# Gated attention scores counted from the middle of 128-token blocks in a two-layer encoder kernel

## The reference, cut to what matters

```python
def gla_scan(q, k, v, g):                      # per head: dk = 128, dv = 256, GLA_CHUNK = 64
    def step(state, inp):
        qc, kc, vc, gc = inp
        gcum = jnp.cumsum(gc, axis=1)
        q_t = qc * jnp.exp(gcum)
        k_t = kc * jnp.exp(-gcum)
        att = jnp.where(causal, jnp.einsum('blhk,bshk->blsh', q_t, k_t), 0.0)
        o = jnp.einsum('blsh,bshv->blhv', att, vc) + jnp.einsum('blhk,bhkv->blhv', q_t, state)
        g_end = gcum[:, -1]
        state = state * jnp.exp(g_end)[..., None] + ...

# gla_mixer: gk is the log gate / 16, q is scaled by 128 ** -0.5, four heads, two directions
o = gla_scan(q, k, v, gk[:, :, 0]) + flip_seq(gla_scan(flip_seq(q), ..., flip_seq(gk[:, :, 1])))
```

## Time and profile before

| what | value |
|---|---|
| median of three runs | 1341.2 us |
| the profiled execution | 1341.43 us, with a span of 1339.6 us |
| PE busy | 1320.0 us, 99% of the span |
| DVE, ACT, POOL busy | 777.4, 641.8, 621.8 us |
| granted PE clock | 0.998 of 2.4 GHz |

### The profile page before, as it was taken

How to read it: one execution, slowest core, us unless ns; L and a number is a source line. 1 busy time by engine, 2 the same in 40 slices (tenths; PEclk the granted TensorE clock), 3 DMA queues, 4 the chain that set the end, 5 groups by cost and what they waited for, 6 DMA issues and landing times.

```text
span 1339.6 us, 16496 instructions
## 1 busy us (share of the span) xinstructions
PE 1320.0 (99%) x6630; PEld 1119.0 (84%) x6630; DVE 777.4 (58%) x890; ACT 641.8 (48%) x1033; POOL 621.8 (46%) x294
## 2 busy tenths in 40 slices
PE   7999999999999999999999999999999999999997
PEld 6878878888898888888889888898998888888887
DVE  5857386840079998885002753386279988882002
ACT  5654787653355444443233576454554544443221
POOL 3344561245424644445553364554535544445551
PEclk9999999999999999999999999999999999999999
DMA  6332111123223332333333223301323333333331
GB/s 206 95 113 85 51 37 40 63 79 98 92 85 103 97 95 94 94 93 100 94 94 103 96 79 95 95 16 63 112 95 95 95 94 98 102 93 88 100 87 63
DMA packets 41452, 119.78 MB, mean 89 GB/s; under 512 B 4384, under 2 KB 12960, under 8 KB 41376
## 3 DMA queue, kind: packets, MB, share of 16 engines
q1 hardware_dynamic: 40160, 116.34, 28.5%
q10 hardware_dynamic: 1216, 2.38, 0.6%
HBM read 116.35 MB, written 2.23 MB: 89 GB/s over the span
## 4 chain that ended last, share of the span: by engine, by line
PE 93%; DVE 4%; ACT 1%; issue 1%; DMA 0%; ACTq 0%; DVEq 0%
PE bank L336 26%; PE bank L337 26%; PE bank L338 26%; PE bank L1774 1%; PE bank L1775 1%; PE bank L1773 1%; PE bank L2077 1%; PE bank L2059 1%; PE bank L1506 1%; PE bank L1509 1%; PE bank L1325 1%; PE bank L387 1%; PE bank L1292 1%; PE bank L1536 1%; DVE sqacc L663 1%
## 5 line engine op out<-in xcount | busy, mean ns | idle before, releaser
L319 POOL TENSOR_TENSOR wlo<-raw,whi 128x1024 fp32r<-128x1024 f32 (+2 forms) x215 | 531.1, 2483 | 633.9 <-ACT whi L313 633.8
L336 PE MATMUL bank<-xw_hi,whi 128*128 128x512 f32 (+1 forms) x1280 | 478.0, 373 | 8.6 <-DVE xw_lo L646 8.1
L338 PE MATMUL bank<-xw_hi,wlo 128*128 128x512 f32 (+1 forms) x1280 | 473.8, 370 | 0.0
L337 PE MATMUL bank<-xw_lo,whi 128*128 128x512 f32 (+1 forms) x1280 | 473.7, 370 | 0.0
L313 ACT ACTIVATE whi<-raw 128x1024 fp32r<-128x1024 f32 (+2 forms) x217 | 221.5, 1025 | 208.0 <-DMA raw<-in_fout 112.2
L336 PEld LDWEIGHTS bank<-xw_hi,whi 128*128 128x128 f32 x1280 | 242.5, 189 | 50.3 <-issue 8.9
L338 PEld LDWEIGHTS bank<-xw_hi,wlo 128*128 128x128 f32 x1280 | 242.3, 189 | 41.1
L337 PEld LDWEIGHTS bank<-xw_lo,whi 128*128 128x128 f32 x1280 | 242.5, 189 | 39.8 <-issue 0.2
L596 DVE RECIPROCAL small<-small 128x2 f32<-128x2 f32 x8 | 1.3, 165 | 315.1 <-ACT small L521 313.7
L715 DVE SCALAR_TENSOR_TENSOR cbuf<-ubuf,par,cbuf 128x510 f32<-128x510 f32 x100 | 168.7, 1687 | 3.5
L711 DVE SCALAR_TENSOR_TENSOR cbuf<-ubuf,par,cbuf 128x510 f32<-128x510 f32 x100 | 144.6, 1446 | 4.7 <-ACT cbuf L844 4.1
(11 more groups left out here) (278 smaller groups left out, 1453.9 us busy)
## 6 DMA issues: line engine op xcount, KB each, us to landing
raw<-in_fin SPq DMA_DIRECT2D x88, 512.0 KB, 3.6
raw<-in_fout SPq DMA_DIRECT2D x32, 448.0 KB, 3.3
raw<-in_gin SPq DMA_DIRECT2D x25, 512.0 KB, 3.6
raw<-in_hin SPq DMA_DIRECT2D x24, 512.0 KB, 3.7
raw<-in_hout SPq DMA_DIRECT2D x16, 512.0 KB, 3.6
raw<-in_fout SPq DMA_DIRECT2D x16, 512.0 KB, 3.6
raw<-in_gout SPq DMA_DIRECT2D x8, 512.0 KB, 3.9
xres<-in_x SPq DMA_DIRECT2D x8, 256.0 KB, 5.8
```

The lines of the kernel that those rows point to most:

```text
L319: engine.tensor_tensor(wlo[s][:, 0:n], raw[s][:, 0:n], whi[s][:, 0:n].bitcast(F32), ALU.subtract).then_inc(w_lo, 1)
L336: first = nc.tensor.matmul(out_ap, wh, ah, start=start, stop=False)
L337: nc.tensor.matmul(out_ap, wh, al, start=False, stop=False)
L338: return first, nc.tensor.matmul(out_ap, wl, ah, start=False, stop=stop)
```

## The change

It has five parts.

1. The running sum `gl` of every gate is counted from the middle of each 128-token block and no longer from the start of each 64-token chunk: `dve_from_middle` copies the eight chunk ends into `ends` (new L1848) and subtracts them from the chunks on one side of the middle (new L1852). One set of keys then serves all 128 queries of its block. The copies `kk`, their carries and zeros go. `dve_keys` is one multiplication into `ek` (new L1949), `scores` has two matmuls of 128 query columns and one cross matmul a request (all new L1991), and `dve_carries` is one addition.
2. Six buffers of `qt`, `ek` and `qx` where there were four (`AHEAD`). The exponentials of pairs 4 and 5 are written in stage gin, behind the split of one weight block, and POOL makes the queries of pairs 0 to 5 there, one pair after each of the last six blocks.
3. The factor 128 ** -0.5 is no longer in the mask and the copy, but in the exponent of `qt`, as a bias in a spare column of `small`, set by a memset.
4. Direction 1's diagonal scores go into `att` with `copy_predicated` under a mask, two instructions where there were two multiplications and two additions. The masks are 1 + identity (upper triangle with 2 on the diagonal) and the strict lower triangle.
5. The order on ACT in stage gla: three cross copies come before the table of Exp, and `outs(0)` is taken apart. Some semaphores are merged (`wgk_in`, `gmask_in`, `tri_in` into `gla_in`; `rope_in` into `cst_in`; `last_t` into `last_x`; `last_stored` into `out_stored`).

```diff
+AHEAD = 6
         def dve_gate_weights(dve):
-            dve.wait_ge(sem("wgk_in"), 16)
+            dve.wait_ge(sem("gla_in"), 48)
...
         def pe_hin(pe):
-                    pe.wait_ge(sem("cst_in"), 16)
+                    pe.wait_ge(sem("cst_in"), 32)
...
         def act_gin(act):
-            act.wait_ge(sem("carry_set"), CARRIES)
+            act.wait_ge(sem("carry_set"), 2)
             nc.scalar.activation(carry[:], carry[:], ACT.Exp, scale=GK_NORM).then_inc(sem("carry_exp"), 1)
+            act.wait_ge(sem("gate_mid"), G0)
             for n in range(4):
+                act_gate_exps(act, n)
+            his(act, base + 1 + 2 * G0)
+            for n in range(4, AHEAD):
                 act_gate_exps(act, n)
...
+        def dve_from_middle(dve, t):
+            d = t // GLA_HEADS
+            at, last = slice(t * NREQ * NCH, (t + 1) * NREQ * NCH), 0 if d else CH - 1
+            dve.wait_ge(sem("gate_scan"), t + 1)
+            nc.vector.tensor_copy(ends[:, at].unsqueeze(2), chunks_of(t)[:, :, last:last + 1]).then_inc(
+                sem("gate_ends"), 1)
+            dve.wait_ge(sem("gate_ends"), t + 1)
+            early = chunks_of(t)[:, d::2]
+            nc.vector.tensor_tensor(early, early, ends[:, at][:, d::2].unsqueeze(2).broadcast_to([P, NREQ * NCH // 2, CH]),
+                                    ALU.subtract).then_inc(sem("gate_mid"), 1)
...
         def dve_gin(dve):
                     if t >= GLA_HEADS:
                         least(t, ft)
+                    if ft:
+                        dve_from_middle(dve, t - 1)
                     dve.wait_ge(sem("gate_act"), 3 * t + 3)
                     dve.wait_ge(sem("gate_min"), t + 1)
                     nc.vector.tensor_tensor(ubuf[0][:], ubuf[0][:], cbuf[1][:], ALU.subtract).then_inc(
...
         def dve_keys(dve, n):
+            nc.vector.tensor_tensor(ek[n % AHEAD][:], ck(gqkv, 4 + n // 2), ek[n % AHEAD][:], ALU.mult).then_inc(
+                sem("gla_kk"), 1)
...
         def pe_gla(pe):
-                    for c in range(NCH):
-                        s = c // 2
-                        nc.tensor.matmul(out[:, s * SEQ + c * CH:s * SEQ + (c + 1) * CH],
-                                         kks(n)[:, r, c * SEQ + s * P:c * SEQ + (s + 1) * P],
-                                         qt[n % 4][:, r * SEQ + c * CH:r * SEQ + (c + 1) * CH], start=True, stop=True)
...
+                    for s in range(2):
+                        against(s, qt[n % AHEAD][:, r * SEQ + s * P:r * SEQ + (s + 1) * P], s)
+                    last = against(d, of_request(qx[n % AHEAD], r, P), 1 - d)
...
         def dve_gla(dve):
+                        nc.vector.copy_predicated(own[r], mask, blocks(sbank(d, r)[:])).then_inc(sem("gla_db"), 1)
```

More of the change, by code:

```diff
@@ L131, in build_program @@
         with ExitStack() as s:
-            kk1 = sb("kk1", NREQ * NCH * SEQ, F32, s)
+            sb("to_cbuf2", 2 * T, F32, s)
+            qx4, qx5 = (sb(f"qx{i}", NREQ * P, F32, s) for i in (4, 5))
         cbuf = [sb(f"cbuf{i}", T) for i in range(4)]
@@ L1869, in dve_gin @@
+        def dve_carries(dve):
+            dve.wait_ge(sem("gate_ends"), G0)
+            nc.vector.memset(small[:, 6:7], math.log(QG)).then_inc(sem("carry_set"), 1)
+            by_chunk = ends[:].rearrange("p (i c) -> p i c", c=NCH)
+            nc.vector.tensor_tensor(carry[:].unsqueeze(2), by_chunk[:, :, 1:2], by_chunk[:, :, 2:3], ALU.add).then_inc(
+                sem("carry_set"), 1)
         def dve_gin(dve):
@@ L1977, in dve_zero_keys @@
-        def dve_zero_keys(dve, n):
-            d = n % 2
-            for c in ((0, 2) if d == 0 else (1, 3)):
-                s0 = CH * (c + 1) if d == 0 else CH * (c - 1)
-                nc.vector.memset(kks(n)[:, :, c * SEQ + s0:c * SEQ + s0 + CH], 0.0).then_inc(sem("kk_zero"), 1)
+            if n >= AHEAD:
+                act.wait_ge(sem("gla_s"), n - AHEAD + 1)
+            f = slice((d * GLA_HEADS + hd) * T, (d * GLA_HEADS + hd + 1) * T)
+            nc.scalar.activation(qt[n % AHEAD][:], gl[:, f], ACT.Exp, bias=small[:, 6:7], scale=GK_NORM).then_inc(sem("gla_e"), 1)
@@ L1995, in dve_keys @@
-            step = SEQ + CH
-            if d == 0:
-                own = kks(n)[:, :, 0:3 * step].rearrange("p r (c y) -> p r c y", y=step)[:, :, :, 0:CH]
-                first, other = 0, 3
-            else:
-                own = kks(n)[:, :, CH:].rearrange("p r (c y) -> p r c y", y=step)[:, :, :, SEQ:]
-                first, other = 1, 0
-            for to, c in ((own, slice(first, first + 3)),
-                          (kks(n)[:, :, other * step:other * step + CH].unsqueeze(2), slice(other, other + 1))):
-                nc.vector.tensor_tensor(to, k[:, :, c], e[:, :, c], ALU.mult).then_inc(sem("gla_kk"), 1)
```

214 lines of the change are left out of this document (67 added, 147 removed).

## The result

The changed kernel takes 1333.48 us in the median of 4 runs (1333.04 to 1334.40), the kernel before 1341.01 beside it (1340.36 to 1341.83): a ratio of 0.9944, 95% interval 0.9932 to 0.9956, clear of no change. Five more runs of it gave 1333.86. I had given 1335.8, with 1334.2 as the lower end. The profiled run took 1333.35 us, its span is 1331.5 (1339.6 before).

The account below looks back on a forecast made before the run. PE, busy for 99% of the span, was taken to bound the kernel. 1341.43 - 6.6 (gla: 6.2 scores, 0.4 waits) + 1.1 (gate 3) = 1335.9, given as 1335.8 for a median; range 1334.2 to 1338.5.

Parts of the forecast that it names:

- Scores: PE's scores in gla: a request falls from 1.12 to 0.72 us, leaving PE 6.2 us less to do.
- The passage of 0.17: PE's scores: the time from one request's last record to the next request's start, 0.17 us against steps of 0.11.
- Rival 2: All 96 score records: 128 columns cost twice the 64, 0.21 us, so the time is 1343.2; chance 0.04.
- The predicated copy: DVE in gla: a predicated copy of 256 elements takes 0.38 us like the masking multiplication, bounds 0.3 and 0.7.
- Waits in gla: PE in gla: new waits of 0.4 us against 0.8 that go, so waits give back 0.4 us.
- Gate 3: PE in gin: a new wait of 1.1 us for gate 2's minimum, since POOL's split delays DVE's scan; bounds 0 and 3.4.
- rival 1: DVE's scan gets the seam ahead of POOL's split, so no wait at gate 3: 1334.7 us; chance 0.14.
- The collision at 775 to 777: DVE in gin: the new subtraction meets POOL's split of 775.50 to 777.91 and ends at about 778.4.
- Edits at no cost: End of gin, pairs 4 and 5's exponentials, POOL's queries, bias, masks, semaphores, ACT's order: 0 us, 0.2 either way.

Follow-up runs that it names:

- e5: Changed kernel with direction 1's own scores placed by a masking multiplication and an addition instead of the predicated copy: 1335.21 us, 0.9961 of the kernel before.
- e1: Changed kernel with each 128 x 128 diagonal score matmul issued as two of 64 columns: 1340.30 us, 0.9995 of the kernel before.
- e3: Changed kernel with a 128 x 256 memset, some 0.27 us, ahead of gate 1's own subtraction on VectorE: 1334.80 us, 0.9955 of the kernel before.
- e6: Changed kernel with four buffers instead of six, pairs 4 and 5 prepared in stage gla again: 1334.76 us, 0.9955 of the kernel before.
- e2: Changed kernel with the copy of the ends and the middle's subtraction moved behind a gate's scan: 1336.22 us, 0.9966 of the kernel before.
- f3: Changed kernel with five matmuls on the tile of ones before TensorE's first operands: 1332.81 us, 0.9944 of the kernel before.
- f1: Changed kernel with gla's copies and scores waiting for one request instead of two, and nine matmuls on ones at the start: 1332.36 us, 0.9944 of before.
- e4: Changed kernel with gla's cross copies and next scores waiting for one request instead of both: 1333.05 us, 0.9941 of the kernel before.

## Why the prediction was off

- **Scores: mechanism right, a term mis-sized.** I predicted 0.72 us a request and a gain of 6.2; it is 0.67 and 7.1. The spacing of 0.11 was right (0.112). The passage of 0.17 from one request to the next was misread: I had taken the first step of L2063's two records as 0.11 and given the rest to the passage. It is the other way round, 0.165 inside L2063 and 0.112 to the next start, already in the kernel before, and in the new form every step is 0.112.
- **Rival 2, wide matmuls that aren't cheap: refuted.** Records of 128 columns are spaced by 0.112 and records of 64 by 0.112 too; my 0.105 was a mean with the one short step of 0.055 in it. By the table in the Trainium skill, "TensorE: Matmul & The Clock Gate", section "Back-to-back issue gap", the scores would have become 7% longer; they took 40% less. The same section says ahead of its table that in a stream with a load of weights for each matmul both set the spacing, and the records fit that: with 128 fresh weights each, 64 columns come no faster than 128. That the loads are what holds them back was not tried by itself.
- **The predicated copy: right.** 0.78 a pair against 0.76 forecast. With the addition in its place e5's stage is 2.4 us longer.
- **Waits in gla: wrong in detail.** I had new waits of 0.4 against old ones of 0.8. Since a pair takes 1.34 and not 1.45 beside a chain of 1.6, they are 0.78, and with what follows each of them 1.0 both before and after (e1): no gain. So the stage came out 7.16 shorter and not 6.6, with 0.9 more from the scores and 0.4 less from the waits.
- **Gate 3: the step that failed.** The step was "now POOL's split is waiting when the subtraction ends, gets the turn": a wait of 1.1 us. Measured: no wait, rival 1. The collision at 775 to 777 was right, its end too late. I let the middle's subtraction end 0.5 us after POOL and gate 1's own 0.7 later. Measured, the held subtraction is over 0.28 after POOL's end at 777.02, and the next starts 0.07 before that: own subtraction done at 777.91, where I had 779.1 - 0.9 = 778.2 on the clock of this run. Of the cover of 0.27 us that the scan had before, 0.02 was left. e3 took that away and got the wait. Having weighed it at 0.14, I was far too sure of a race that my own estimates could not resolve: their error (0.3) was as large as the margin that I had reckoned with (0.26, from 778.84 to 779.1).
- **Edits at no cost: right.** Behind values 3 both traces are 430.6 us long, and from gate 0 to pair 0 they differ by 0.05. PE has no wait for POOL's splits at block 20 or 21.
- **Range.** Without the wait the forecast is 1334.7, still within the range; it took the mis-sized scores as well to end below it. My own bounds allowed for both: 1335.8 - 1.1 - (7.7 - 6.2) = 1333.2. I let the lower end stop at 1334.2, as if only one of the two could come.
- **Outside the change.** The profiled run of before was 0.9 us behind at the start by the moment at which the clock rose, and I took its own time as the base. Against medians this is worth about 0.4 us (1341.43 against 1341.06).

Counted again: 1341.43 - 7.1 (scores) + 0 (waits) + 0 (gate 3) - 0.9 (start) = 1333.4; the profiled run took 1333.35. Of the error of 2.3 us against the median, 1.1 are gate 3, 0.6 the stage (7.16 against 6.6), and the remaining 0.6 lie within what the start does from run to run.

## What to carry to other kernels

On a saturated TensorE count records: with 128 fresh weights each, four matmuls of 64 columns took twice what two of 128 took. Once that stage is shorter, each bank's chain is to be laid against the new time of a pair, since most of an addition or a table load that was covered before is then paid (e5, e6). A short VectorE instruction with its operands in SBUF costs what GpSimd's running instruction still has to go (2.30 us for a copy of eight elements in e2), so it belongs ahead of a wait that exists anyway, and not behind a scan in which GpSimd's next instruction arrives. When the outcome hangs on who is first at a seam by less than the error of the sum, each side gets about half the chance.

## What the hardware showed beside that

- The moment at which TensorE's records at the start go from 0.213 to 0.12 us apart lay between 11.2 (e5) and 13.5 us (before) in the nine profiled runs that gave TensorE no work before them; the granted clock of the changed kernel's profile reads 1.00 there all the same, and only the spacing shows it. In f3 the granted clock shows it too.
- The same at the end: in every profile the granted clock falls to the lower level near the end, as a rule behind PE's last record. In e1 it fell at 1330.2, in the last eight records, and in e6 before the last of them (1.58 us instead of 1.16): their traces are 1.1 and 0.4 us longer behind values 3 than the changed kernel's. Seven of e1's eleven executions have a mean granted clock of 0.997 and took 1340.02 to 1341.14 us; the four with 0.998 took 1339.50 to 1340.00. In f1 the two executions over 1334 are those with 0.997. In e4 and e6 the times do not sort that way.
- Another source of scatter: at about 756 us PE waits 0.3 to 0.4 us for a reduction of DVE in six of thirteen profiled runs, of before and after alike. From block 1 to gate 0 it is 749.98 us in the changed kernel's profile, with the wait, and 749.33 in e1's, without it. With the start, this is as large as the 1.4 us between the fastest and the slowest run of the changed kernel; that it makes them was not tried.
- VectorE and GpSimd at a seam: whichever had arrived when the other ended went on, in the changed kernel with a lead of 0.02 us; what stood behind it then lost 2.1 us (e3's scan) or 1.0 us (the split, 3.41 instead of 2.40). VectorE's instructions that read a bank did not take part: in the changed kernel's profile the scalings took 0.66 to 0.69 us, the minima 0.74 to 0.75 and the predicated copies 0.43 to 0.45 each, with a GpSimd instruction beside them or not.
